# Expert layer of a two-block transformer on one core: experts ordered by load, weights loaded once per expert, small units in two products

## The reference

```python
def moe_swiglu(h, w_router, b_router, w_gate, w_up, w_down):
    logits = (h @ w_router).astype(F32) + b_router.astype(F32)
    top_logits, top_idx = lax.top_k(logits, TOP_K)
    top_w = jax.nn.softmax(top_logits, axis=-1)
    gates = jnp.sum(jax.nn.one_hot(top_idx, N_EXPERTS, dtype=F32) * top_w[..., None], axis=-2)
    for e in range(N_EXPERTS):
        y_e = swiglu(h, w_gate[e], w_up[e], w_down[e])
        out = out + gates[..., e:e + 1] * y_e
```

## Time and profile before

| | |
|---|---|
| median of 3 runs | 2874.41 us (2869.45 to 2878.86) |
| first listed time | 2878.86 us |
| span of the profiled execution | 2878.7 us |
| PE busy | 2756.1 us, 96% |
| DVE busy | 2185.2 us, 76% |
| ACT busy | 1703.5 us, 59% |
| HBM read | 686.53 MB, 239 GB/s over the span |
| issues of expert pieces | 462 of 1024 KB |

### The profile page before, as it was taken

The page is one execution under the profiler, slowest core; times in us unless marked ns, Lnnn a source line. Parts: engine busy times, 40 slices in busy tenths (PEclk is TensorE's granted clock), DMA queues, the critical chain, the costliest instruction groups (busy, mean ns, idle before and its releaser), DMA issues.

```text
span 2878.7 us, 43981 instructions
## 1 busy us (share of the span) xinstructions
PE 2756.1 (96%) x18492; PEld 2453.9 (85%) x18492; DVE 2185.2 (76%) x2158; ACT 1703.5 (59%) x1785; POOL 116.2 (4%) x112
## 2 busy tenths in 40 slices
PE   7778999998999999999999999999999999989998
PEld 6667999987998888888888888888888799989998
DVE  7885655565737888888888888888888668766777
ACT  5314553456646677776767777777776565445543
POOL 7350000000000000000000000000000000000000
PEclk9889999999999999999999999999999999999999
DMA  5103445542527999999999999999999545534553
GB/s 201 60 2 103 159 153 187 187 150 89 162 89 290 343 352 356 347 348 348 359 339 355 349 350 354 346 353 353 347 357 352 199 138 177 190 117 147 176 182 127
DMA packets 238004, 690.42 MB, mean 240 GB/s; under 512 B 10608, under 2 KB 169456, under 8 KB 178416
## 3 DMA queue, kind: packets, MB, share of 16 engines
q1 hardware_dynamic: 235728, 685.52, 66.3%
q10 hardware_dynamic: 2080, 2.10, 0.2%
HBM read 686.53 MB, written 1.05 MB: 239 GB/s over the span
## 4 chain that ended last, share of the span: by engine, by line
PE 74%; DVE 10%; DMA 6%; ACT 5%; issue 3%; DVEq 1%; POOL 0%; POOLq 0%; ACTq 0%; SPq 0%
PE ps L803 22%; PE ps L805 21%; PE ps L804 21%; DMA ring<-moe 5%; DVE w_lo L3394 2%; DVE w_lo L1767 2%; PE ps L1605 1%; DVE more_lo L3394 1%; ACT arena L1736 1%; PE ps L841 1%; ACT w_hi L1751 1%; PE ps L1657 1%; PE ps L1046 1%; PE ps L950 1%; DVEq L2496 1%
## 5 line engine op out<-in xcount | busy, mean ns | idle before, releaser
L1767 DVE TENSOR_TENSOR w_lo<-ring,w_hi 128x1024 fp32r<-128x1024 f32 x362 | 446.5, 1249 | 264.9 <-ACT w_hi L1751 258.8
L1751 ACT ACTIVATE w_hi<-ring 128x1024 fp32r<-128x1024 f32 x362 | 379.8, 1057 | 384.4 <-PE ps L805 364.2
L1739 ACT ACTIVATE w_hi<-ring 128x2048 fp32r<-128x2048 f32 x232 | 445.3, 1919 | 174.5 <-DMA ring<-moe 160.6
L3394 DVE TENSOR_TENSOR w_lo<-ring,w_hi 128x2048 fp32r<-128x2048 f32 x232 | 523.0, 2285 | 27.9 <-ACT w_hi L1739 27.2
L803 PE MATMUL ps<-x_hi,w_hi 128*128 128x256 f32 x1600 | 459.9, 287 | 16.3 <-DVE w_lo L1767 7.4
L804 PE MATMUL ps<-x_lo,w_hi 128*128 128x256 f32 x1600 | 454.4, 284 | 0.0
L805 PE MATMUL ps<-x_hi,w_lo 128*128 128x256 f32 x1600 | 454.3, 284 | 0.0
L803 PEld LDWEIGHTS ps<-x_hi,w_hi 128*128 128x128 f32 x1600 | 308.5, 193 | 22.8 <-issue 16.9
L804 PEld LDWEIGHTS ps<-x_lo,w_hi 128*128 128x128 f32 x1600 | 308.6, 193 | 0.4
L805 PEld LDWEIGHTS ps<-x_hi,w_lo 128*128 128x128 f32 x1600 | 308.5, 193 | 0.0
L1739 ACT ACTIVATE more_hi<-ring 128x2048 fp32r<-128x2048 f32 x115 | 220.8, 1920 | 122.8 <-DMA ring<-moe 117.1
(11 more groups left out here) (402 smaller groups left out, 5541.0 us busy)
## 6 DMA issues: line engine op xcount, KB each, us to landing
ring<-moe SPq DMA_DIRECT2D x347, 1024.0 KB, 6.5
more_raw<-moe SPq DMA_DIRECT2D x115, 1024.0 KB, 6.9
ring<-ffn_w_up SPq DMA_DIRECT2D x44, 1024.0 KB, 5.1
ring<-ffn_w_down SPq DMA_DIRECT2D x22, 1024.0 KB, 4.8
ring<-xa_w_kv SPq DMA_DIRECT2D x16, 1024.0 KB, 5.5
ring<-w_in SPq DMA_DIRECT2D x16, 1024.0 KB, 7.0
ring<-da_w_qkv SPq DMA_DIRECT2D x12, 1024.0 KB, 5.2
ring<-ff_w_gate SPq DMA_DIRECT2D x11, 1024.0 KB, 5.3
```

The source lines that it names most:

```text
L1739: return nc.scalar.activation(o, i, ACT.Copy, **kw)
L1751: nc.scalar.activation(w_hi[:, half_slot(at, half), :], ring[:, s_, half * 1024:half * 1024 + 1024], ACT.Copy).then_inc(hi_ready, 1)
L1767: nc.vector.tensor_tensor(w_lo[:, i, :], ring[:, s_, half * 1024:half * 1024 + 1024], w_hi[:, i, :], ALU.subtract).then_inc(lo_ready, 1)
L3394: nc.vector.tensor_tensor(lo, raw_piece(n), hi, SUB).then_inc(piece_lo, 1)
```

## The change

The experts are ordered by load on DVE (a key of count x 16 - number, compared with every other). Place p of the order of work takes the expert of rank RANKS[p], and a rank has as many units of up to 128 tokens as it can need at most. There are eight places of seven turns, 56 turns and 336 pieces; a piece is used for both units of its place before it is given back. SP reads the eight experts into registers ahead of the first piece. A unit that can have at most 64 tokens is packed: the high parts of its tokens are columns 0 to 63 of the stationary operand and the low parts columns 64 to 127, and two matmuls (with the weights' high and low part) take the place of three; rows 64 to 127 of the result are then added to rows 0 to 63. Side jobs move between the up product and the down product and use free gate banks or the other pair of result banks; the transposes go into the bank of the up product, between the two halves of the gate product.

```diff
+RANKS = (0, 3, 1, 7, 2, 4, 5, 6)
+def units_of_rank(rank):
+    most = 2 * S // (rank + 1)
+    if most <= 64:
+        return [(0, True)]
+    if most <= P:
+        return [(0, False)]
+    return [(0, False), (P, most - P <= 64 and rank > 0)]
...
+def sides_of(g):
+    place, f = divmod(g, PER_SLOT)
+    if place == 0 and f == 0:
+        return [("turn", u, 0) for u in PLACES[0]]
+    if place and f in (1, 2):
+        return [("scatter", place - 1, 2 * f - 2 + i) for i in range(2)]
+    ahead = PLACES[place + 1] if place + 1 < NE else []
+    if f == 3:
+        return [("turn", u, 0) for u in ahead]
+    if f in (4, 5):
+        return [("gather", u, half) for u in ahead[f - 4:f - 3] for half in range(2)]
+    return []
...
             sp.wait_ge(chunk_used, at.n["chunk"])
+            sp.wait_ge(slots_known, 1)
+            known = [sp.value_load(expert_of[0:1, units[0]:units[0] + 1], min_val=0, max_val=NE - 1)
+                     for units in PLACES]
...
+            def products(u, o, x, weights, start, stop):
+                if is_packed(u):
+                    mm(o, x[0], weights[0], start=start, stop=False)
+                    return mm(o, x[0], weights[1], start=False, stop=stop)
+                return three(o, x, weights, start, stop)
...
             def gate(g):
+                pe.wait_ge(side_free, SIDES_BEFORE[g])
+                last_work = works(g)[-1][0]
+                if last_work > 1:
+                    pe.wait_ge(gate_silu, last_work - 1)
+                columns(g, 0, first_piece(g), gate_bank)
+                if g:
+                    turn(g - 1)
+                columns(g, 1, first_piece(g), gate_bank)
...
             def up(g):
+                last_work = works(g)[-1][0]
+                if last_work > 1:
+                    pe.wait_ge(turned_lo, last_work - 1)
...
             for g in range(TURNS):
                 gate(g)
                 up(g)
+                sides(g)
                 if g:
                     down(g - 1)
...
             def gate_to_silu(g):
                 act.wait_ge(piece_used, first_piece(g) + 2)
+                for w, u in works(g):
+                    rows = slice(0, 64 if is_packed(u) else P)
+                    src = ps[:, gate_bank(w), :]
+                    if is_packed(u):
+                        act.wait_ge(turned, w - 1)
+                        copy(prod[0:64, w % 2, :], ps[64:128, gate_bank(w), :]).then_inc(low_rows_out, 1)
+                        act.wait_ge(gate_joined, packed_before(w) + 1)
+                        src = silu[:, w % 2, :]
+                    elif w > 1:
+                        act.wait_ge(prod_done, w - 1)
+                    activate(silu[rows, w % 2, :], src[rows, :], ACT.Silu).then_inc(gate_silu, 1)
...
+            for u in PLACES[0]:
+                for half in range(2):
+                    copy_side(("gather", u, half), first_side_bank(u, half))
+            for n in range(3):
+                high(n)
             for g in range(TURNS):
+                n = first_piece(g)
+                if g and g % PER_SLOT == 1 and g > PER_SLOT:
+                    y_to_high(g // PER_SLOT - 1)
+                high(n + 3)
+                if g:
+                    high(n + 4)
+                    turned_high(g - 1)
+                gate_to_silu(g)
+                if g:
+                    high(n + 5)
+                n = first_piece(g + 1)
+                if g + 1 < TURNS:
+                    high(n)
+                    up_rows(g)
+                    high(n + 1)
...
+                for i, which in enumerate(sides_of(g)):
+                    copy_side(which, side_bank(g, i))
+                if g + 1 < TURNS:
+                    high(n + 2)
...
+            stt(dve, key, ps[:, 3, 2 * NE:3 * NE], 16.0, cst("number"), MUL, SUB)
+            tt(dve, above, repeated(key, [P, NE, NE]), scalars(key, [P, NE, NE]), ALU.is_gt)
+            nc.vector.reduce_sum(position, above, AX)
+            dve.drain()
+            tt(dve, of_unit, repeated(position, wide), scalars(cst("unit_rank"), wide), ALU.is_equal)
+            tt(dve, picked, of_unit, repeated(cst("number"), wide), MUL)
+            nc.vector.reduce_sum(number, picked, AX)
+            dve.drain()
+            nc.vector.tensor_copy(expert_of[:, :], number).then_inc(slots_known, 1)
...
             for g in range(TURNS):
+                n = first_piece(g)
+                if g > PER_SLOT and g % PER_SLOT == 1:
+                    y_to_low(g // PER_SLOT - 1)
+                low(n + 2)
+                low(n + 3)
+                if g:
+                    low(n + 4)
+                    turned_low(g - 1)
+                join_gate(g)
+                if g:
+                    low(n + 5)
+                if g + 1 < TURNS:
+                    low(first_piece(g + 1))
...
+                product(g)
+                for i, which in enumerate(sides_of(g)):
+                    take_side(which, side_bank(g, i))
+                if g % PER_SLOT == 2 and g // PER_SLOT + 1 < NE:
+                    for u in PLACES[g // PER_SLOT + 1]:
+                        build_selection(u)
+                low(first_piece(g + 1) + 1 if g + 1 < TURNS else PIECES - 1)
```

More of the change, by code:

```diff
@@ L139, with units_of, is_packed, is_pair @@
 SMALL_W = LAYERS_AT + 2 * LAYER_W
+WIDE = 512
+PER_SLOT = FFE // WIDE
+TURNS = NE * PER_SLOT
+PIECES = 6 * TURNS
+RAWS, SPLITS = 4, 4
+RANKS = (0, 3, 1, 7, 2, 4, 5, 6)
[6 more added lines that the diff above has]
+    return [(0, False), (P, most - P <= 64 and rank > 0)]
+UNITS = [(place, shift, packed) for place, rank in enumerate(RANKS) for shift, packed in units_of_rank(rank)]
+PLACES = [[u for u, unit in enumerate(UNITS) if unit[0] == place] for place in range(NE)]
+LAST = len(UNITS) - 1
+def units_of(g):
+    return PLACES[g // PER_SLOT]
+def is_packed(u):
+    return UNITS[u][2]
+def is_pair(g):
+    return len(units_of(g)) == 2
+FIRST_WORK = [sum(len(units_of(i)) for i in range(g)) for g in range(TURNS + 1)]
+def works(g):
+    return [(FIRST_WORK[g] + i, u) for i, u in enumerate(units_of(g))]
+def packed_before(w):
+    return sum(is_packed(u) for g in range(TURNS) for j, u in works(g) if j < w)
 def shape_constants():
@@ L213, in down_piece @@
     return 6 * g + 8 if g < TURNS - 1 else PIECES - 2
[L216 to L227, removed]
+def sides_of(g):
[10 more added lines that the diff above has]
+    return []
+SIDES = [("gather", u, half) for u in PLACES[0] for half in range(2)]
+SIDES_BEFORE = []
+for _g in range(TURNS):
+    SIDES_BEFORE.append(len(SIDES))
+    SIDES += sides_of(_g)
+SIDE_AT = {which: n + 1 for n, which in enumerate(SIDES)}
 def expert_pieces(gate, up, down):
@@ L1616, in scatter @@
                 for t in range(2):
                     cs = slice((2 * part + t) * P, (2 * part + t + 1) * P)
[L1618 to L1629 removed]
+                    o = ps[:, bank, t * S:(t + 1) * S]
@@ L1651, in turn @@
[L1651 to L1659, removed]
+                        last = products(u, ps[:, bank_of(w), :], (xs[0][:, xk, :], xs[1][:, xk, :]),
+                                        (hi[:, k, :], lo[:, k, :]), xk == 0, xk == KT - 1)
@@ new lines, in columns, with turn @@
+                last.then_inc(piece_used, 1)
+            def turn(g):
+                for w, u in works(g):
+                    rows = 64 if is_packed(u) else P
+                    pe.wait_ge(prod_done, w + 1)
+                    for q in range(4):
+                        last = nc.tensor.transpose(ps[:, up_bank(w), q * P:q * P + rows],
+                                                   prod[0:rows, w % 2, q * P:(q + 1) * P],
+                                                   cst("ident", 0, rows)[0:rows, :])
+                    last.then_inc(turned, 1)
@@ L1661, in down, with sides @@
+            def sides(g):
+                for i, (what, n, part) in enumerate(sides_of(g)):
+                    if is_pair(g):
+                        pe.wait_ge(gate_silu, works(g)[i][0] + 1)
+                    if what == "turn":
+                        turn_selection(n, side_bank(g, i))
+                    if what == "gather":
+                        gather(n, part, side_bank(g, i))
+                    if what == "scatter":
+                        scatter(n, part, side_bank(g, i))
             def down(g):
-                s, f = divmod(g, PER_SLOT)
@@ L3506, in dve_moe @@
[L3506 to L3530 removed]
+            tt(dve, first, first, second, ADD)
```

414 lines of the change are left out of this document (200 added, 214 removed).

## The result

The changed kernel takes 2828.92 us (median of 4 runs, 2825.76 to 2831.88) against 2875.6 of the kernel before; the ratio is 0.9836, 95% interval 0.9824 to 0.9849. That is 47 us less, where the forecast was 21 less (2853): the direction was right and 2829 lies in the range of 2826 to 2878, but the saving that was forecast is less than half of the one measured. The profiled execution has a span of 2824.1 us.

A forecast was written before the change was run, and what follows sets the result against it. TensorE was taken as the bound, transfers just behind. Place 4 -38.6, place 3 +12, ready pieces -3, pair turns -3, single full turns 0, start +11.7: -21 us, 2853 on the median; range 2826 to 2878.

The forecast's parts named there:

- ready pieces: Entering place 3 from a pair turn, three or four pieces already lie ready, worth 3 us less.
- start: Before the first expert matmul: fetches must await the expert order, +11.7 us, with ends of +7 and +18.
- rest of the stage: Single full turns 0 (bounds -4, stalls go, to +28); pair turns -3, their share of 12 us of stalls.
- rival D: Whole launch: time follows bytes, 126 x 2.97 = 375 us less, 2500 us; chance 0.01.
- The chain in place 3: Each packed turn: DVE's join waits behind a split, ACT's Silu and next split wait for it; DVE stands still 2.7 us.
- the 19.5: Forecast length in us of one packed turn in place 3, taken from 20.0 since operations overlap a little.
- the forecast's own case: Whole launch: the terms as summed, -21 us to 2853, range 2843 to 2868; chance 0.58.
- rival C: Place 3 runs at the transfers' pace, 17.5 us a turn: total -36, 2838 us; chance 0.20.
- part 2: Place 3, two products for three: pieces and the join set the pace, +12 us (ends -3 and +36).
- the 125.1: PE's us for an average slot of seven three-product turns, with two half gathers, four scatter parts and one selection.
- Rival A: Place 3: PE stays at 1.2 GHz, some 23 us a turn, +36 for +12, total +3, 2877 us; chance 0.12.
- Rival B: Single full turns: transfers set the pace, 19.2 us a turn, +38, total +17, 2891 us; chance 0.09.

The follow-up runs named there:

- the kernel before with the spare columns: The kernel before with 150 unused columns behind its constants, moving later buffers 600 bytes as in the changed kernel, no instruction changed: 2867.76 us, ratio 0.998.
- with the chain cut: The changed kernel with ACT splitting the next down piece before it waits for the joined gate, in place 3's seven turns: 2821.03 us, ratio 0.9819.

## Why the prediction was right in direction and wrong in size

The runs split the change into parts that can be laid beside the sum. The offsets and the two packings are differences of medians: before 2874.2, with the new offsets 2867.8, with order and single loads 2867.0, with place 4 packed 2831.5, with place 3 packed 2830.3. The start and the rest of the stage are read from the traces of the kernel before with the spare columns and of the run with all units in three products, which have the same offsets.

| part | predicted | measured |
|---|---|---|
| place 4, two products | -38.6 | -35.4 |
| place 3, two products | +12, and -3 for ready pieces | -1.3 |
| start | +11.7 | +10.2 and some 2 at the low clock |
| rest of the stage | -3 | -11.7 |
| buffers' offsets | 0 | -6.5 |
| sum | -21 | -43 |

The medians alone give 44. By the intervals, a difference of two medians is uncertain by some 5 us, so the table tells the large parts apart, and not 1 us from 3.

**What held.** TensorE as the bound: half the bytes of the whole stage took off 10 us of 2875, and rival D fell with it. The 0.230 us a matmul: by starts it is 0.2303 before, after, and with all units in three products. The turns of every kind of place within 0.3 us. The start: order known 2.4 us after the counts, eight reads in 4.8 us, gathers in 9.9 instead of 8.8, hidden landing, the low clock behind the wait. The chain in place 3, and the 19.5. That 2829 fell inside the range is luck: it lies outside the range of the forecast's own case (2843 to 2868), and the low end of the whole range was made of rival C, which did not come true.

**The step that failed most is the comparison in part 2**, "7 x 19.5 = 136.5 against 125.1: +12". The 19.5 was right and the 125.1 was the wrong thing to set it against. An average slot holds one gather pair and one scatter, 6.1 us; place 3 holds 12.2, work that leaves other places and that a PE with three products would have to do there too. With three products the place is not 125.1 but 115.9 + 3.1 + 12.2 = 131.2 us, and the run shows PE busy in it throughout. So the term should have been some +3 and not +12 (by the traces +2.1), and the 3 us for ready pieces take it to nothing; the two measured -1.3 together, against +9 in the sum. The forecast was 10 us too high by this step.

**The rest of the stage** is the second miss: it was taken as -3 and is -11.7 (the stage goes from 1394.0 to 1384.4 us although it now holds the 2 us at the low clock, which the table has under the start). The forecast found 12 us of stalls in the stage and let only the pair turns' share go, 3 us. They were for the most part delays behind late pieces: with half the bytes the stage of the kernel before is 7 to 14 us shorter. Without the second loads they went everywhere, in the single full turns too, where the text had taken 0 and named -4 as the end. Whether there the fewer transfers or the new order of the splits did it, no run separates. Against this stand 4.6 us of new waits: 1.35 us at the end of each of the three pair places, for the turned low parts, and 0.5 us early in the first. One unit's gather less lies behind the first expert matmul, since two are gathered ahead of it (31.4 us for 34.0; its price is in the start, where I had counted it, but not its absence here). The transposes cost the same: 0.88 us for a batch of eight, 0.44 for four. The last wait of 3.43 us and the 1.2 GHz behind it are 1.41 us in all other runs of the kernel before too, so this is not the change's doing; in the trace with the spare columns a wait of 3.54 us at 1899.59, with the low clock behind it, stands in its place. The stage of the kernel before varies from one execution to the next: 1394.0, 1394.0, 1394.4 and, with 24 bytes, 1387.1 us.

**The offsets** are a third miss, 6.5 us: the text costed only the columns' instructions, and said nothing of what moves when a tensor grows. No row of the trace before could have given the size; that `m_hi` moves could have been read from the listing.

**Rival A** (place 3 at 1.2 GHz): the clock of place 3 was 0.96, between 1.00 and 0.91 in stretches of 20 us, three of six at 0.91. PE waited there 1 to 3 us several times and was busy 81% of the stretch. Behind three of these waits, 2.61, 2.68 and 2.64 us long, 3 to 7 starts are 0.43 us apart, and then the full clock is back; behind another of 2.61 us and one of 3.28 us none are:

```profile
1571.39 0.50 PE L1701 MATMUL ps<-more_hi,act_hi 128*128 128x512 f32 x1 [2.68 <-DVE more_lo L3508]
1571.72 0.55 PE L1702 MATMUL ps<-more_lo,act_hi 128*128 128x512 f32 x1
1572.08 0.63 PE L1701 MATMUL ps<-more_hi,act_hi 128*128 128x512 f32 x1
1572.50 0.63 PE L1702 MATMUL ps<-more_lo,act_hi 128*128 128x512 f32 x1
...
1628.22 0.50 PE L1701 MATMUL ps<-w_hi,act_hi 128*128 128x512 f32 x1 [3.28 <-DVE w_lo L3508]
1628.56 0.40 PE L1702 MATMUL ps<-w_lo,act_hi 128*128 128x512 f32 x1
```

The rule of the Trainium skill ("TensorE: Matmul & The Clock Gate", section "HAM oscillation") holds here for the waits of 3.43 and 4.90 us, which put PE to 1.2 GHz, and in place 3 only now and then; the clock did not stay down. **Rival B** (single full turns slower): 1980 to 2080 has PE busy 100 of 100 us. **Rival C**: place 3 did not run at the transfers' pace as changed; with the chain cut it came to 18.2, against 17.5.

## What to carry to other kernels

Ask of each stretch which engine is full before counting bytes: 126 transfers of 1 MB fewer bought some 10 us of short waits while TensorE was full, and the start, which now has to know the order first, took them back; 168 matmuls fewer bought 35 us in one place and 1 in another, depending on what stood right behind TensorE there. When one unit is compared with an average one, take side work out of both or put the same into both. And a tensor that grows moves its neighbours: repeat the kernel before with the new layout and nothing else before giving the whole difference to the change.

## What was not expected of the hardware

The spacing of fp32r matmuls of 256 columns was 0.1187 or 0.1136 us with the same instructions, by a shift of 600 bytes of the buffer that holds the stationary operand; 24 and 1024 bytes left it at 0.1187, and 32 bytes gave 0.1174. Within the expert stage the spacing of 512-column matmuls with `x_hi`/`x_lo` stationary was 0.228 with weights in `w_hi`/`w_lo` and 0.232 to 0.233 with weights in `more_hi`/`more_lo`, in the kernel before and in the changed one, and the same with half the bytes transferred. With the second unit's tokens stationary, in a buffer of their own (`more_x_hi`), it was nearly the other way round in the changed kernel: 0.230 and 0.228. So it is the pair of buffers that goes with the spacing, and not the one of the weights alone. What in the addresses decides is open.
